# A hybrid mixer block: three moves in the written order of ScalarE and TensorE

## The reference, cut to what matters

```python
def hybrid_layer(x, ...):
    proj = rms_norm(x, ln1) @ w_in            # 23 slabs of 128 columns
    mq, mk, mv, sq, sk, sv, xqk, xv, xo, xi, xf = split(proj)
    # 1. MoBA attention, 6 heads: head norm and rope on mq, mk, causal softmax
    # 2. mLSTM, 4 heads: qk = silu(causal_conv(xqk)); gates xi, xf
    #      num = (q k^T * w_intra) v ; den = sum(q k^T * w_intra)
    #      h = num / max(|den|, exp(-m)) ; y = rms_norm(h * sigmoid(xo))
    # 3. sliding window attention, 6 q heads, 2 kv heads: norm, rope, softmax with sinks
    x = x + concat([y_moba, y_mlstm, y_swa]) @ w_out
    return x + square(relu(rms_norm(x, ln2) @ w_up)) @ w_down
```

## Time and profile before

| what | value |
|---|---|
| time, median of 3 | 1441.41 us (1440.87 to 1442.11) |
| profiled execution, its own time | 1441.39 us |
| its span in the profile | 1439.4 us |
| mean granted TensorE clock | 0.997 |
| TensorE matmul busy | 1411.2 us, 98% |
| VectorE busy | 1146.1 us, 80% |
| ScalarE busy | 827.7 us, 58% |
| mixer of layer 0, from its gate branch to its last transposes | about 42 to 136 us |
| mixer of layer 1, the same | about 353 to 447 us |

### The profile page before, as it was taken

How to read it: one execution, slowest core, us unless ns; L and a number is a source line. 1 busy time by engine, 2 the same in 40 slices (tenths; PEclk the granted TensorE clock), 3 DMA queues, 4 the chain that set the end, 5 groups by cost and what they waited for, 6 DMA issues and landing times.

```text
span 1439.4 us, 25521 instructions
## 1 busy us (share of the span) xinstructions
PE 1411.2 (98%) x10325; PEld 1314.2 (91%) x10325; DVE 1146.1 (80%) x1800; ACT 827.7 (58%) x1248; POOL 10.5 (1%) x21
## 2 busy tenths in 40 slices
PE   7999999999999999999999999999999999999997
PEld 7898888889888888889999999998899999999986
DVE  7888888888798888887778777777787787778763
ACT  5776776445776875344656655444446575554542
POOL 2000000000000000000000000000000000000000
PEclk9999999999999999999999999999999999999999
DMA  9643999986545999988854578798787445778661
GB/s 251 165 140 93 282 265 270 300 221 168 140 129 169 279 257 304 279 250 221 219 147 140 173 232 233 214 250 227 223 235 213 147 145 171 233 214 225 185 185 65
DMA packets 485364, 297.13 MB, mean 206 GB/s; under 512 B 14956, under 2 KB 455792, under 8 KB 485120
## 3 DMA queue, kind: packets, MB, share of 16 engines
q1 hardware_dynamic: 483728, 292.00, 71.4%
q10 hardware_dynamic: 816, 1.84, 0.4%
q0 software_dynamic: 704, 1.66, 0.4%
HBM read 289.43 MB, written 1.05 MB: 202 GB/s over the span
## 4 chain that ended last, share of the span: by engine, by line
PE 73%; DVE 13%; ACT 6%; issue 4%; DMA 3%; SPq 1%; DVEq 0%; ACTq 0%
PE acc L1923 11%; PE acc L1924 11%; PE acc L1925 11%; PE mx L1940 9%; PE acc L1940 8%; PE mx L1941 5%; DVE w_lo L1068 4%; PE acc L1941 4%; ACT w_hi L577 2%; DVE ada_acc L1158 2%; DMA raw<-in_w_in 1%; SPq L434 1%; PE acc L1955 1%; PE acc L1956 1%; PE acc L1957 1%
## 5 line engine op out<-in xcount | busy, mean ns | idle before, releaser
L1068 DVE TENSOR_TENSOR w_lo<-raw,w_hi 128x1024 fp32r<-128x1024 f32 x450 | 541.5, 1220 | 114.0 <-ACT w_hi L577 112.0
L577 ACT ACTIVATE w_hi<-raw 128x1024 fp32r<-128x1024 f32 x450 | 458.3, 1049 | 139.2 <-DMA raw<-in_w_in 85.1
L1923 PE MATMUL acc<-h,w_hi 128*128 128x258 f32 (+1 forms) x1776 | 508.4, 286 | 6.1 <-DVE w_lo L1068 3.8
L1924 PE MATMUL acc<-h,w_hi 128*128 128x258 f32 (+1 forms) x1776 | 503.6, 284 | 0.0
L1925 PE MATMUL acc<-h,w_lo 128*128 128x258 f32 (+1 forms) x1776 | 498.0, 280 | 0.0
L1923 PEld LDWEIGHTS acc<-h,w_hi 128*128 128x128 f32 x1776 | 335.0, 189 | 13.5 <-issue 5.1
L1925 PEld LDWEIGHTS acc<-h,w_lo 128*128 128x128 f32 x1776 | 338.2, 190 | 0.0
L1924 PEld LDWEIGHTS acc<-h,w_hi 128*128 128x128 f32 x1776 | 335.7, 189 | 2.6 <-issue 2.4
L1940 PE MATMUL mx<-u,w_hi 128*128 128x512 f32 x864 | 304.2, 396 | 0.1
L1941 PE MATMUL mx<-u,w_lo 128*128 128x256 f32 x864 | 241.3, 279 | 0.0
L1940 PEld LDWEIGHTS mx<-u,w_hi 128*128 128x128 f32 x864 | 162.1, 188 | 37.5 <-DVE u L1872 0.4
(11 more groups left out here) (291 smaller groups left out, 1652.8 us busy)
## 6 DMA issues: line engine op xcount, KB each, us to landing
raw<-in_w_in SPq DMA_DIRECT2D x132, 512.0 KB, 4.2
ada<-in_w_ada SPq DMA_DIRECT2D x96, 512.0 KB, 5.1
raw<-in_w_ffn_in SPq DMA_DIRECT2D x88, 512.0 KB, 4.5
raw<-in_w_up SPq DMA_DIRECT2D x64, 512.0 KB, 5.6
raw<-in_w_down SPq DMA_DIRECT2D x64, 512.0 KB, 5.8
raw<-in_w_out SPq DMA_DIRECT2D x32, 512.0 KB, 4.2
raw<-in_w_ffn_out SPq DMA_DIRECT2D x32, 512.0 KB, 4.2
raw<-in_w_ret_o SPq DMA_DIRECT2D x16, 512.0 KB, 4.1
```

What stands on the lines that cost most here:

```text
L577: nc.scalar.activation(w_hi[:, n % NS], raw[:, n % NS], ACT.Copy).then_inc(hi_ready, 1)
L1068: V.tensor_tensor(w_lo[:, n % NS], raw[:, n % NS], w_hi[:, n % NS].bitcast(F32), ALU.subtract).then_inc(lo_ready, 1)
L1923: mm(outp, w_hi[:, i % NS, k], rhs[:, k, 0], start=k == 0, stop=False)
L1924: mm(outp, w_hi[:, i % NS, k], rhs[:, k, 1], start=False, stop=False)
```

## The change

ScalarE: the copy to `ebc` moves in front of `conv_silu()` and of the table load behind it; the rounding of identity and masks in layer 0 becomes a step of its own behind `weights(0)`. TensorE, in each of the two layers: `out_bank(0, 0)` moves in front of the wait for `qk_r` and `sums(4)`; `out_bank(2, 3)` and `out_bank(3, 2)` move from behind `at_outputs(2)` to the place between `turn(2)` and `at_scores(4)`. No instruction is added or removed on any engine.

```diff
--- before.py
+++ after.py
@@ -652,11 +652,12 @@
                 def spread_exp():
                     act.wait_ge(f_uc, l + 1)
                     nc.scalar.activation(ebc[:], mx[:, 0], ACT.Copy).then_inc(f_bcsb, 1)
-                    if l == 0:
-                        act.wait_ge(s_con, 32)
-                        act.wait_ge(s_mask, 16)
-                        nc.scalar.activation(ident_r[:], ident, ACT.Copy)
-                        nc.scalar.activation(masks[:], mask_raw[:], ACT.Copy).then_inc(m_ready, 1)
+
+                def masks_rounded():
+                    act.wait_ge(s_con, 32)
+                    act.wait_ge(s_mask, 16)
+                    nc.scalar.activation(ident_r[:], ident, ACT.Copy)
+                    nc.scalar.activation(masks[:], mask_raw[:], ACT.Copy).then_inc(m_ready, 1)
 
                 def conv_silu():
                     act.wait_ge(cv_ready, l + 1)
@@ -793,10 +794,12 @@
                 ahead(15)
                 spread_max()
                 ahead(16)
+                spread_exp()
                 conv_silu()
                 nc.scalar.preload_act_table_set(LOG_EXP)
-                spread_exp()
                 weights(0)
+                if l == 0:
+                    masks_rounded()
                 ahead(18)
                 head_square(1)
                 weights(1)
@@ -2214,9 +2217,9 @@
                 pe.wait_ge(at_e, l * 6 + 2)
                 at_scores(2)
                 at_outputs(0)
+                out_bank(0, 0)
                 pe.wait_ge(qk_r, l * 5 + 4)
                 sums(4)
-                out_bank(0, 0)
                 out_bank(0, 1)
                 pe.wait_ge(qk_r, l * 5 + 5)
                 values(2)
@@ -2237,11 +2240,11 @@
                 out_bank(2, 2)
                 pe.wait_ge(at_y, l * 6 + 2)
                 turn(2)
+                out_bank(2, 3)
+                out_bank(3, 2)
                 pe.wait_ge(at_e, l * 6 + 4)
                 at_scores(4)
                 at_outputs(2)
-                out_bank(2, 3)
-                out_bank(3, 2)
                 out_bank(3, 0)
                 out_bank(3, 1)
                 pe.wait_ge(at_y, l * 6 + 3)
```

## The result

The changed kernel takes 1442.81 us (median of 22 runs, 1440.31 to 1447.59) where the kernel before takes 1441.15 (22 runs, 1438.42 to 1445.81). The ratio is 1.0013 with an interval of 1.0007 to 1.0019, some 1.9 us slower (1.0 to 2.7). Forecast were 1439.3 us and a range up to 1440.9: the sign is wrong and the time lies outside the range.

The account below looks back on a forecast made before the run. TensorE is busy 1411.2 of 1439.4 us, but VectorE leads in the attention part. Gains 0.95 + 1.06 + 0 + 2 x 0.03 = 2.07 us off 1441.39 gave 1439.3 us, range 1437.0 to 1440.9.

Parts of the forecast that it names:

- The copy in front of the silu: ScalarE's `ebc` copy ahead of the silu: `ml_scores(0)` 1.16 and 1.06 us earlier, lasting gain 0.95 and 1.06.
- rival 4: At `ml_scores(0)` the silu replaces the copy as what is waited for: 1440.2 us, within the forecast's own spread.
- rival 2: Copy's lead lost by `turn(2)`, VectorE or partner moves not following: gain 0 to 1 us, 1440.9; chance 0.09.
- The quarter in front of `sums(4)`: Six matmuls ahead of `sums(4)`: cost 0; bounds +0.2 us in layer 0, -0.6 in layer 1.
- Two quarters in front of `at_scores(4)`: Twelve matmuls fill TensorE's 1.23 us hole, which moves to `turn(3)`: -0.03 us per layer, bounds +0.2 and -1.23.
- The sign that the prediction named for its account: On VectorE in the attention part, `outputs(4)` stays as far behind `outputs(1)` as before, 16.7 us.
- The rest of that step: VectorE leads the attention part; TensorE idles about 1.1 us at `turn(3)`, and 0.03 us of lead remains at `turn(5)`.
- Rival 3: `sums(4)` 0.72 us late heads the chain through `head_norm(4)` and `rope(4)` to `at_scores(4)`: slower, 1443.2 us; chance 0.04.
- Rival 1: All five TensorE holes in the mixers close: 5.1 us, 1436.3; half way 1437.3; chance 0.13 for both.

Follow-up runs that it names:

- experiment 1: Kernel before with only ScalarE's part (copy to `ebc` ahead of the silu, masks rounded behind `weights(0)`): 1438.86 us against 1440.58, ratio 0.9990.
- 9: Kernel before with only ScalarE's part of the change, measured a second time: 1439.52 us against 1441.75, ratio 0.9987.
- 3: Changed kernel with `out_bank(3, 2)` back behind `at_outputs(2)`, `out_bank(2, 3)` left ahead of `at_scores(4)`: 1439.11 us against 1440.58, ratio 0.9986.
- experiment 8: Changed kernel with `out_bank(2, 2)` and `out_bank(2, 3)` ahead of `at_scores(4)`, `out_bank(3, 2)` back behind `at_outputs(2)`: 1438.88 us against 1441.75, ratio 0.9985.
- experiment 5: Kernel before with only `out_bank(0, 0)` moved in front of `sums(4)`: 1440.84 us against 1441.39, ratio 1.0003.
- experiment 4: Changed kernel with VectorE making slab 26's `w_lo` in front of `rope(4)` instead of behind it: 1441.16 us against 1440.58, ratio 1.0003.
- experiment 2: Kernel before with only `out_bank(2, 3)` and `out_bank(3, 2)` moved in front of `at_scores(4)`: 1444.41 us against 1440.58, ratio 1.0025.
- 7: Changed kernel unaltered, measured and profiled a second time: 1443.41 us against 1441.39 for the kernel before, ratio 1.0012.

## Why the prediction was wrong

**The copy in front of the silu: right.** `ml_scores(0)` comes 1.16 and 1.07 us earlier against the gate rows (forecast 1.16 and 1.06), and `ml_outputs(1)`, at 70.36 with a layer that began 0.71 us later, is 0.95 earlier, as worked out. Experiments 1 and 9 have a gain of 0.10 and 0.13%, 1.4 and 1.9 us (0.1 to 2.7 and 0.6 to 3.2), beside the 2.01 forecast. The silu didn't take the copy's place (rival 4): neither `ml_scores(0)` has idle time ahead of it. The lead was not eaten (rival 2): in experiment 1 `at_outputs(5)` is 1.01 and 0.85 earlier, and in 3, 8 and 9, which have the copy too, 0.67 to 1.21; in 5, which has not, 0.07.

**The quarter in front of `sums(4)`: right**, by experiment 5 and its distances; the time alone could not show a cost within the bounds of +0.2 and -0.6.

**Two quarters in front of `at_scores(4)` (next to nothing): this step failed.** I worked out when twelve matmuls would be through, 118.0 to 118.3, as if they waited for nothing but TensorE. The description ahead of it says that a quarter needs only its slab and the finished head chunk, and leaves out that the slab's `w_lo` has to be made by VectorE. `out_bank(w, b)` begins with a wait for `lo_ready` of its own slab, and for `out_bank(3, 2)` this is slab 26. In its old place, behind `at_scores(4)` and `at_outputs(2)`, it found it done: in layer 0 before, the `w_lo` was through at 117.99 + 1.23 = 119.22, and the quarter, behind `at_outputs(2)` and the other one, began at 121.05. In the new place the wait stands ahead of `at_scores(4)`, and the engine that ends it has `rope(4)` in its queue first. The hole I wanted to fill ends with `rope(4)`; the filler can't begin before the step behind `rope(4)` is done. So with VectorE's order as it is it cannot lie in that hole, whatever its length; experiment 4, with the order turned, puts it there and pays on VectorE. The bound of +0.2 for the step covered twelve matmuls that overrun, not a wait.

The size: `at_scores(4)` 2.03 us later behind `rope(4)` in both layers, in the three profiles with the edit and `w_lo` behind `rope(4)` (after, experiments 2 and 7), and 0.00 to 0.04 in all others. In the profile of the changed kernel it adds up: layer 0, `rope(4)` 0.69 earlier, then 2.03 lost, then 0.24 more (below), together 1.58 (93.44 less 91.86); layer 1, 0.93 earlier, 2.04 lost, 0.10 regained, together 1.01. With the forecast 2.01 of the copy against 2 x 2.03 it makes +2.05 us; measured 1.9 (1.0 to 2.7). The sign that the prediction named for its account, `outputs(4)` as far behind `outputs(1)` as before (16.7 us), failed by about that amount: 18.99 us in layer 0 of the changed kernel and 18.66 in layer 1.

**The rest of that step held, and made the loss stick.** From `at_scores(4)` to `at_outputs(5)` the ring takes 16.40 us before and 16.39, 16.39, 16.31 and 16.32 in experiments 1, 3, 2 and 7 (layer 0): VectorE leads, and a late start at `maxima(4)` is handed through to the end of the mixer. TensorE's idle time in front of `turn(3)` came as foreseen (0.96 in layer 1, forecast 1.1). The same rigidity that made me cost the filling of the hole at nothing makes a delay at its head cost full price.

**Rivals.** Rival 3 named the right sign but another place; experiments 3 and 5 exclude it, and that its 1443.2 lies close to the 1442.81 measured is chance. Rival 1, all holes close, is excluded by experiment 8: with the hole in front of `at_scores(4)` closed by ready work the time is that of the copy alone. The section Optimization Strategy of the Trainium skill's "Perfetto Trace Analysis" says to find what blocks the gap and make that come sooner. The trace agrees where that was done (the copy: `ml_scores(0)` 1.16 and 1.07 us sooner) and shows no gain for work put into the gap (experiment 8). What I had not done is the same question for the filler: what does it wait for itself?

## What to carry to other kernels

Call releaser the engine whose signal ends a wait. A piece of work moved into an idle stretch of an in-order engine takes its own waits along, and they then stand in front of everything behind it. Before costing it, write down each semaphore it waits on, who signals it, and where that step stands in the releaser's order: if the releaser makes it behind the very step that ends the stretch, the filler cannot lie in it. A wait that the trace of before does not show at a step proves only that the step was late enough, not that it waits for nothing. Ready filler in a stretch set by another engine was worth nothing that could be measured here; moving the releaser's step (the copy) was worth all of the gain.

## What the runs showed of the hardware

In layer 0 of the changed kernel's profile TensorE's granted clock fell to 0.50, its lower level of 1.2 GHz, for some 3 us. The view of stretches (time; then busy share and count of PE, PEld, DVE, ACT and POOL, granted clock, DMA share, GB/s):

```profile
120.00:121.00 1.00, 1.00 (x11) 0.75 (x11) 0.00 (x0) 0.00 (x0) 0.00 (x0) 1.00 1.19 299
121.00:122.00 1.00, 1.00 (x8) 0.35 (x6) 0.14 (x1) 0.00 (x0) 0.00 (x0) 0.50 0.41 97
122.00:123.00 1.00, 1.00 (x12) 0.90 (x10) 0.96 (x2) 0.00 (x0) 0.00 (x0) 0.50 0.00 0
123.00:124.00 1.00, 1.00 (x7) 0.77 (x4) 0.86 (x5) 0.65 (x4) 0.00 (x0) 0.50 0.00 0
```

Before it the engine had been idle for 1.72 us and had then, from 119.30 on, run the sixteen matmuls of the quarter and of `at_scores(4)`; the stretch from 120 to 121 us still has full clock, 1.00. The twelve of `at_outputs(2)` took 1.55 us where they took 0.88 in layer 1, and from `at_scores(4)` to `at_outputs(5)` layer 0 took 16.64 us against 16.30: about 0.3 us. Layer 1 had an idle stretch of 1.73 us at the same place and kept its clock, and the profiles of experiments 2 and 7 have 16.3 us there as well. So the fall is not a fixed cost of such a wait; what decides it stays open.

The partner moves land at times that vary from execution to execution without a change in the steps ahead of them: VectorE's wait at `rope(3)` in layer 0 was 1.00 us before and 0.33 in experiment 2, which has the same code up to there; in layer 1, whose own steps are the same up to there too, the wait at `rope(2)` was 1.13 us before and absent in experiment 2. `rope(4)` ended 0.70 and 1.03 us earlier in its two layers. A single profile cannot show an effect of 1 us in this kernel's mixer; distances between two neighbouring steps can, and the medians of 7 to 29 runs, whose intervals are 0.9 to 1.6 us either way, resolve hardly less than that. The changed kernel's profile also began layer 0 with 0.71 us more behind it than that of before, and regained 1.3 us behind the second mixer. The first arose ahead of the changed steps. As for the second, the time from the last `at_outputs(5)` to the end lies between 992.2 and 995.8 us over the eleven profiles (993.7 before, 992.5 after) and does not go with the change; its cause stays open.
